# Half of each expert's second matrix product in three fp32r passes instead of native fp32

## The chip, the cores and the metric

The kernel runs on one core of a Trainium2 chip. The metric is device time in microseconds (us) of one execution. The engines named below are TensorE (PE, its weight loads PEld), VectorE (DVE), ScalarE (ACT), GpSimd (POOL) and SyncE (SP, which here only issues transfers).

## The reference

One forward pass over 512 tokens of width 1024: a first block (four token mixers, a gated merge, a mixture of experts) and then two layers of a second block. The change lies in the mixture of experts. Cut to what matters:

```python
def one_seq(xs):                                   # 512 x 1024
    lg = (xs @ wr_g) + br_g                        # 4 groups, the best is taken
    le = ((xs @ wr_e) + br_e)                      # 8 experts in the group, the best 2 are taken
    ...
    hg = jnp.einsum('sd,edh->seh', xs, w_gate)     # 32 experts, 1024 -> 256
    hu = jnp.einsum('sd,edh->seh', xs, w_up)
    h = jax.nn.silu(hg) * hu * gate[..., None]
    return jnp.einsum('seh,ehd->sd', h, w_down)    # 256 -> 1024
```

Each token has two experts with weight, so the kernel computes only those.

## The kernel before

`moe` sorts the 1024 token-expert pairs into 39 **blocks** of at most 128 rows: one per expert, and 7 overflow blocks for experts with more than 128 rows, which are empty when none has. For block b it gathers the rows (`gather`, POOL), and loads the expert's matrices from HBM: gate and up together as two chunks of 1 MB (`load_g`, chunks 2b and 2b+1), and the down matrix as one of 1 MB (`load_d`).

Products of fp32 precision are made in two ways here. Gate and up use **three fp32r passes**: each operand is split into a high part (ACT copies it with rounding to fp32r: `rounds` L1926 for weights, `round_rows` L1937 for tokens) and a low part (DVE subtracts: `split` L2103, `split_rows` L2109), and PE sums high x high, high x low, low x high (L1853 to L1855). The down product (`down`, L1867 to L1878) takes the loaded matrix as it is, in **native fp32**: two halves of 512 output columns, banks 4 and 5, each with two matmuls. A native fp32 matmul shows as two records in the trace.

Every engine runs its own list in program order; the loops over b are written out. In iteration b:

- PE: `gate_up(b)` (24 matmuls), `turn_rows(b+1)` (8 transposes, L1864), `down(b-1)`, `turn_hidden(b)` (2 transposes into bank 6, L1883). `down(b-1)` waits until ACT (`y_out_low`, L1943) and DVE (`y_out_high`, L2116) have emptied banks 4 and 5 of block b-2, since these banks are single.
- ACT: SiLU (L1961), `round_rows(b+1)`, `rounds(2b+4)`, `rounds(2b+5)`, `y_out_low(b-1)`.
- DVE: SiLU times up (`mid`, L2125), `split_rows(b+1)`, `split(2b+4)`, the copy of the turned hidden rows out of bank 6 (`hid`, L2131), `split(2b+5)`, `y_out_high(b-1)`.
- SP: `load_d(b+2)` (L1752) waits for the end of `down(b-1)`, and behind it in the queue stand the two chunks of `load_g(b+3)` (L1745). So the three 1 MB transfers of a block are issued together, just as a `down` ends; their chunks are rounded and split one iteration later.
- POOL: an indirect gather of rows three blocks ahead and a scatter of the results to HBM.

In this document a **period** runs from the end of one `down` to the end of the next; the trace marks these ends by SP's issues of L1752.

Of the kernel before, what the change touches and what calls it, by code (L numbers as in the profile page):

```python
# [38 lines left out]
OVERFLOW = 2 * SEQ // (ROWS + 1)  # L39
BLOCKS = EXPERTS + OVERFLOW  # L40
# [236 lines left out]

@contextmanager
def memory(k, **shapes):

    with ExitStack() as ctx:
        out = []
        for name, shape in shapes.items():
            dt = F32
            if shape[0] in ("r", "i"):
                dt, shape = (F32R if shape[0] == "r" else mybir.dt.int32), shape[1:]
            k.tensors += 1
            out.append(ctx.enter_context(k.nc.sbuf_tensor(f"{name}_{k.tensors}", [128, *shape], dt)))
        yield out[0] if len(out) == 1 else out
# [1382 lines left out]
def moe(k, gain1, bias1, gain2, bias2):  # L1672
# [12 lines left out]
    four = lambda name: const(k, name).rearrange("p (q e) -> p q e", q=4)  # L1685
    norm_names = norm_programs(k, k.res, gain1, bias1, k.eps[:, 0:1], True, (None,) * 5, out=k.res)[0]
    with memory(k, raw=(3, CHUNK), work=(13 * SEQ,), gh=("r", 2, KT * ROWS), gl=("r", 2, KT * ROWS), xtm=(4, D),
                router=(KT, 36), lg=(4, 36), pick=(4, 4), m=(4, 8), le=(4, 32), wide=(4, 32), hot=(2, 4, 32),
                gates=(2, 4), mask=(4, 32), rank=(4, 32), per=(4, 32), cmp=(OVERFLOW, 32), at=(6, 8),
                slot=(2, BLOCKS), stats=(4, 12), moments=(4, 4), ids=("i", 2, BLOCKS), extra=("i", 8)) as (  # L1690
            raw, work, gh, gl, xtm, router, lg, pick, m, le, wide, hot, gates, mask, rank, per, cmp, at, slot,
            stats, moments, ids, extra), \
            stage(k, "router_in", "logits_ready", "exp_ready", "best_ready", "rows_turned", "rows_out", "rows_stored",
                  "mask_ready", "ranks_ready", "places_ready", "slots_ready", "ids_ready", "vector_order",
                  "g_loaded0", "g_loaded1", "g_loaded2", "g_loaded3", "d_loaded0", "d_loaded1", "d_loaded2",
                  "g_rounded", "g_split", "g_used", "x_cleared", "gathered0", "gathered1", "gathered2",
                  "x_turned", "x_rounded", "x_split", "hidden_ready", "silu_ready", "mixed", "turned",
                  "turned_copied", "y_ready", "y_low", "y_high", "scattered0", "scattered1", "picked_in0", "picked_in1", "picked_in2", "picked_in3", "summed_y",
                  "rstd_done", "normed", "back_turned", "res_ready", "res_ready2", "tail_square_used", "tail_log_ready", "squared_rows", "params_in", *norm_names, drained=True) as (
                block, router_in, logits_ready, exp_ready, best_ready, rows_turned, rows_out, rows_stored,  # L1700
                mask_ready, ranks_ready, places_ready, slots_ready, ids_ready, order,
                g_loaded0, g_loaded1, g_loaded2, g_loaded3, d_loaded0, d_loaded1, d_loaded2,
                g_rounded, g_split, g_used, x_cleared, gathered0, gathered1, gathered2,
                x_turned, x_rounded, x_split, hidden_ready, silu_ready, mixed, turned,
                turned_copied, y_ready, y_low, y_high, scattered0, scattered1, picked_in0, picked_in1, picked_in2, picked_in3, summed_y,
                rstd_done, normed, back_turned, res_ready, res_ready2, square_used, log_ready, squared_rows, params_in, *norm_sems):
        nrm = work[:, :].rearrange("p (a n) -> p a n", n=SEQ)
        norm = norm_programs(k, k.res, gain1, bias1, k.eps[:, 0:1], True,
# [4 lines left out]
        g_hi = [ws.hi[:, 0, :], ws.hi[:, 1, :], flat(k.xh, 0), flat(k.xh, 1)]  # L1713
        g_lo = [ws.lo[:, 0, :], ws.lo[:, 1, :], flat(k.xl, 0), flat(k.xl, 1)]
        d_raw = [raw[:, 2, :], flat(k.res, 0), flat(k.res, 1)]
        g_loaded = [g_loaded0, g_loaded1, g_loaded2, g_loaded3]
        d_loaded = [d_loaded0, d_loaded1, d_loaded2]
        gathered = [gathered0, gathered1, gathered2]
        scattered = [scattered0, scattered1]
        picked_in = [picked_in0, picked_in1, picked_in2, picked_in3]  # L1720
        x_rows = [work[:, D * s:D * s + D] for s in range(3)]
        y_rows = [work[:, D * s:D * s + D] for s in (3, 4)]
# [8 lines left out]
        tile = lambda t: slice(128 * t, 128 * t + 128)  # L1731
# [82 lines left out]
        def _(pe):  # L1814
# [52 lines left out]
            def down(b):  # L1867
                pe.wait_ge(turned_copied, b + 1)
                pe.wait_ge(d_loaded[b % 3], 16 * (b // 3 + 1))
                if b:  # L1870
                    pe.wait_ge(y_low, b)
                    pe.wait_ge(y_high, b)
                for half in range(2):
                    for u in range(2):
                        last = pe.matmul(k.bank[4 + half][:, :], hid[b % 2][:, tile(u)],
                                         d_raw[b % 3][:, D * u + SEQ * half:D * u + SEQ * half + SEQ],
                                         start=u == 0, stop=u == 1)
                    last.then_inc(y_ready, 1)  # L1878
# [39 lines left out]
        def _(act):  # L1918
            def rounds(c):
                act.wait_ge(g_loaded[c % 4], 16 * (c // 4 + 1))  # L1920
                if c >= 4:
                    if c % 2:
                        act.wait_ge(hidden_ready, (c - 4) // 2 + 1)
                    else:
                        act.wait_ge(g_used, (c - 4) // 2 + 1)
                act.activation(g_hi[c % 4], g_raw[c % 4], ACT.Copy).then_inc(g_rounded, 1)  # L1926
# [5 lines left out]
            def round_rows(b):  # L1932
                for half in range(2):
# [2 lines left out]
                        act.wait_ge(hidden_ready, b - 1)  # L1936
                    act.activation(gh[:, b % 2, halves[half]], k.bank[2 + half][:, :], ACT.Copy).then_inc(x_rounded, 1)  # L1937

            def y_out_low(b):
                act.wait_ge(y_ready, 2 * b + 1)  # L1940
                if b >= 2:
                    act.wait_ge(scattered[b % 2], 16 * (b // 2))
                act.activation(y_rows[b % 2][:, 0:SEQ], k.bank[4][:, :], ACT.Copy).then_inc(y_low, 1)  # L1943
# [15 lines left out]
            for b in range(BLOCKS):  # L1959
                act.wait_ge(hidden_ready, b + 1)  # L1960
                act.activation(silu[b % 2], k.bank[b % 2][:, 0:256], ACT.Silu).then_inc(silu_ready, 1)  # L1961
                if b + 1 < BLOCKS:
                    round_rows(b + 1)
                if b + 2 < BLOCKS:
                    rounds(2 * b + 4)
                    rounds(2 * b + 5)
                if b:
                    y_out_low(b - 1)
            y_out_low(BLOCKS - 1)

            def rows_to_features(q):
# [33 lines left out]
        def _(dve):  # L2005
# [117 lines left out]
            for b in range(BLOCKS):  # L2123
                dve.wait_ge(silu_ready, b + 1)
                dve.tensor_tensor(mid[b % 2], silu[b % 2], k.bank[b % 2][:, 256:512], ALU.mult).then_inc(mixed, 1)  # L2125
                if b + 1 < BLOCKS:
                    split_rows(b + 1)
                if b + 2 < BLOCKS:
                    split(2 * b + 4)
                dve.wait_ge(turned, b + 1)  # L2130
                dve.tensor_copy(hid[b % 2], k.bank[6][:, 0:256]).then_inc(turned_copied, 1)  # L2131
                if b + 2 < BLOCKS:
                    split(2 * b + 5)
                if b:
                    y_out_high(b - 1)
            y_out_high(BLOCKS - 1)

            def rows_to_features(q):
# [519 lines left out]
def store_out(k, c0):  # L2658
    ws = k.ws
    end = c0 + LAYERS * LAYER_CHUNKS  # L2660
    with stage(k, "spare0", "spare1", "spare2", "spare3", "spare4", "spare5", "stored") as (block, _, _, _, _, _, _, stored):
        @block.sync
        def _(sp):
            sp.dma_start(k.dram["outT"], k.res[:, :, :]).then_inc(stored, 16)
            sp.wait_ge(stored, 16)
            for c in (end + 1, end + 2):
                sp.wait_ge(ws.loaded[c % SLOTS], 16 * (c // SLOTS + 1))


def build(nc, dram):  # L2670
    with ExitStack() as ctx:
        k = Kernel(nc, dram)
        k.bank = [ctx.enter_context(nc.psum_tensor(f"bank{b}", [128, 512], F32)) for b in range(8)]
        k.ws = Stream(nc, ctx, dram["weights"])
        k.xh, k.xl, k.res, k.consts, k.par1, k.par2, k.mats1, k.mats2, k.eps = ctx.enter_context(memory(
            k, xh=("r", KT, SEQ), xl=("r", KT, SEQ), res=(KT, SEQ), consts=(CONSTS,), par1=(P1_COLS,),
            par2=(P2_COLS,), mats1=(548,), mats2=(256,), eps=(5,)))
# [279 lines left out]
```

## Time and profile before

| | |
|---|---|
| median of 3 runs | 3155.22 us (3152.75 to 3158.64) |
| the profiled execution | 3157.21 us |
| its span, first to last instruction | 3155.0 us |
| granted clock of TensorE, mean | 0.942 |
| PE matmul busy, share of the span | 2813.8 us, 89% |
| DVE, ACT, POOL busy | 1752.9, 703.4, 1339.1 us |
| block loop of `moe` | about 925 to 1329 us of the span |

The profile gives for each instruction its start and length, and for the idle time ahead of it the last event that ended the wait. Busy time alone does not tell which engine sets the pace: in a loop of 39 like blocks the question is which chain of instructions and waits closes on itself once per block, and how long it is. That is read from the order in time of PE, ACT, DVE and SP.

### The profile page before, as it was taken

Reading aid. Unit: us, or ns where it says so; the run is one execution under the profiler, and the core shown is the slowest. Engines: PE = TensorE matmul, PEld = TensorE weight load, DVE = VectorE, ACT = ScalarE, POOL = GpSimd, SP = SyncE. Lnnn points to the kernel's source line nnn. Section 1 sums busy time; section 2 is a strip of 40 time slices with the busy share of each in tenths; the row PEclk is TensorE's granted clock in tenths of the full one; section 3 lists DMA queues with packets and bytes.
Section 4 is the critical chain, followed back from the end, with each engine's and each line's share of the span. In section 5 each row is a group of like instructions: output and inputs, shape, how many; then the busy total and the mean of one; then the engine's idle time right before and its main releaser. Section 6 shows DMA issues by size and latency. Waiting matters only on the chain. (4 is left out here: it accounts for less than half of the span.)

```text
span 3155.0 us, 32794 instructions
## 1 busy us (share of the span) xinstructions
PE 2813.8 (89%) x12686; PEld 2128.1 (67%) x12686; DVE 1752.9 (56%) x2031; ACT 703.4 (22%) x1082; POOL 1339.1 (42%) x382
## 2 busy tenths in 40 slices
PE   7988777879779999879889989999898899989998
PEld 6843436757556666557468867888665688768886
DVE  1176455449366666566644456882356645568841
ACT  1023220021135555452430010000233500110000
POOL 5600000036311111213147757777432277667776
PEclk9989888879979999989999999999999999999999
DMA  4322010033248888622212222222233022222223
GB/s 158 121 103 98 24 58 20 1 113 128 82 156 311 334 309 330 247 97 102 66 54 94 93 80 91 97 94 93 99 109 91 28 94 95 93 80 94 94 98 116
DMA packets 84168, 366.35 MB, mean 116 GB/s; under 512 B 32062, under 2 KB 32446, under 8 KB 45608
## 3 DMA queue, kind: packets, MB, share of 16 engines
q1 hardware_dynamic: 66088, 338.55, 29.6%
q10 hardware_dynamic: 6688, 17.21, 1.7%
q0 software_dynamic: 11232, 8.43, 0.9%
q8 instruction: 104, 1.70, 0.2%
q14 instruction: 56, 0.46, 0.0%
HBM read 364.75 MB, written 36.08 MB: 127 GB/s over the span
## 5 line engine op out<-in xcount | busy, mean ns | idle before, releaser
L177 PE MATMUL bank<-xh,w_hi 128*128 128x512 f32 x1704 | 678.1, 398 | 78.2 <-DVE xl L548 31.7
L133 POOL TENSOR_TENSOR w_hi<-w_raw,w_zero 128x2048 fp32r<-128x2048 f32 x138 | 497.5, 3605 | 588.6 <-PE bank L177 360.8
L179 PE MATMUL bank<-xh,w_lo 128*128 128x512 f32 x1704 | 670.5, 393 | 0.0
L178 PE MATMUL bank<-xl,w_hi 128*128 128x512 f32 x1704 | 670.4, 393 | 0.0
L136 POOL TENSOR_TENSOR w_lo<-w_raw,w_hi 128x2048 fp32r<-128x2048 f32 x138 | 649.5, 4706 | 10.8
L177 PEld LDWEIGHTS bank<-xh,w_hi 128*128 128x128 f32 x1704 | 324.1, 190 | 173.0 <-issue 51.7
L153 POOL TENSOR_TENSOR w_lo<-w_raw,w_hi 128x2048 fp32r<-128x2048 f32 x24 | 111.0, 4625 | 775.2 <-DVE yl L653 519.1
L179 PEld LDWEIGHTS bank<-xh,w_lo 128*128 128x128 f32 x1704 | 324.0, 190 | 68.8
L178 PEld LDWEIGHTS bank<-xl,w_hi 128*128 128x128 f32 x1704 | 324.9, 191 | 65.7 <-issue 0.5
L2649 DVE TENSOR_TENSOR fl<-work,fh 128x512 fp32r<-128x512 f32 x44 | 210.8, 4791 | 1.5
L661 DVE TENSOR_TENSOR part<-sig,bank 128x512 f32<-128x512 f32 x76 | 52.3, 688 | 251.5 <-PE bank L179 250.8
L1801 POOL DMA_INDIRECT picked_rows<-work,ids x39 | 39.2, 1005 | 327.8 <-DVE work L2116 261.4
L231 PE MATMUL bank<-whole_x,w_raw 128*128 128x512 f32 x320 | 150.7, 629 | 2.0 <-PEq L275 2.0
L723 DVE SCALAR_TENSOR_TENSOR res<-res,bank 128x512 f32<-128x512 f32 x32 | 22.0, 688 | 232.0 <-PE bank L179 232.0
L667 DVE TENSOR_TENSOR part<-part 128x512 f32<-128x512 f32 x72 | 148.1, 2057 | 2.5
L2648 DVE CAST fh<-work 128x512 fp32r<-128x512 f32 x44 | 145.7, 3312 | 1.5
L643 ACT ACTIVATE sig<-bank 128x512 f32<-128x512 f32 x76 | 45.6, 600 | 436.3 <-DVE part L661 420.4
L178 PE MATMUL bank<-fl,w_hi 128*128 128x512 f32 x352 | 137.0, 389 | 0.0
L179 PE MATMUL bank<-fh,w_lo 128*128 128x512 f32 x352 | 137.0, 389 | 0.0
L177 PE MATMUL bank<-fh,w_hi 128*128 128x512 f32 x352 | 137.0, 389 | 0.0
L2635 ACT ACTIVATE work<-bank 128x512 f32<-128x512 f32 x44 | 26.4, 599 | 437.7 <-PE bank L179 437.7
L231 PEld LDWEIGHTS bank<-whole_x,w_raw 128*128 128x128 f32 x320 | 63.5, 202 | 84.8 <-issue 84.7
(543 smaller groups left out, 4865.8 us busy)
## 6 DMA issues: line engine op xcount, KB each, us to landing
w_raw<-weights SPq DMA_DIRECT2D x216, 1024.0 KB, 4.8
raw<-weights SPq DMA_DIRECT2D x51, 1024.0 KB, 8.5
res<-weights SPq DMA_DIRECT2D x26, 1024.0 KB, 6.3
early_gates<-gate_rows SPq DMA_DIRECT2D x20, 256.0 KB, 2.1
ahead<-early_gates ACTq DMA_DIRECT2D x20, 256.0 KB, 3.5
distance_bias<-distance_bias_once ACTq DMA_DIRECT2D x8, 512.0 KB
na_bias<-grid_bias SPq DMA_DIRECT2D x16, 240.0 KB, 4.8
strips<-distance_bias SPq DMA_DIRECT2D x8, 448.0 KB, 3.9
```

The lines of the kernel that those rows point to most:

```text
L133: pool.tensor_tensor(self.hi[:, s, :], self.raw[:, s, :], self.zero[:, 0:1].to_broadcast([128, CHUNK]), ALU.add).then_inc(self.rounded, 1)
L136: pool.tensor_tensor(self.lo[:, s, :], self.raw[:, s, :], self.hi[:, s, :].bitcast(F32), ALU.subtract).then_inc(self.split, 1)
L153: engine.tensor_tensor(self.lo[:, s, :], self.raw[:, s, :], self.hi[:, s, :].bitcast(F32), ALU.subtract).then_inc(self.split, 1)
L177: self.released(pe.matmul(out, hi, moving[0], start=start, stop=False))
L178: pe.matmul(out, hi, moving[1], start=False, stop=False)
L179: return pe.matmul(out, lo, moving[0], start=False, stop=stop)
L231: mm = pe.matmul(self.k.bank[self.banks[j]][:, :], self.k.ws.raw[:, c % 2, 128 * (b % 16):128 * (b % 16) + 128], self.x[:, t, :], start=t ...
L643: act.activation(sig[:, l % 2, :], k.bank[l % 4][:, :], ACT.Sigmoid).then_inc(sigmoid_ready, 1)
L661: dve.tensor_tensor(part[:, 0 if n == 0 else 1, :], gate, k.bank[4 + u % 4][:, :], ALU.mult).then_inc(banks_free, 1)
L667: step(dve.tensor_tensor(part[:, 0, :], part[:, 0, :], part[:, 1, :], ALU.add))
L2648: step(dve.tensor_copy(fh[:, j, :], mid[:, 0, :]))
L2649: dve.tensor_tensor(fl[:, j, :], mid[:, 0, :], fh[:, j, :].bitcast(F32), ALU.subtract).then_inc(halved, 1)
```

## The change

In `down(b)` the first half (columns 0 to 511, bank 4) is computed in three fp32r passes, and the second half stays native fp32. Its operands are split per block. ACT rounds half of the down matrix, 128x1024 elements (`round_down`, into `d_hi`), and the turned hidden rows, 128x256 (`round_hidden`, into `hid_hi`). DVE subtracts both (`d_lo`, `hid_lo`). All four buffers are single, so each is written only when the first half of the `down` before has ended. `down(b)` waits for both new splits before either of its halves. The native copy `hid` stays, for the second half.

To make room, the small routing tables (`le`, `wide`, `mask`, `rank`, `per`, `hot`) become views of `work`, which is free at that time. Five semaphores move from the stage to the whole kernel, and six unused ones of `store_out` go.

```diff
+        first_half = lambda b: d_raw[b % 3].rearrange("p (u n) -> p u n", u=2)[:, :, 0:SEQ]
+        table = lambda n, w=128: work[:, 5 * D + n:5 * D + n + w].rearrange("p (q e) -> p q e", e=32)
+        le, wide, mask, rank, per = (table(128 * n) for n in range(5))
+        hot = table(640, 256).rearrange("p (a q) e -> p a q e", a=2)
...
@@ tensor: down(b)
+                pe.wait_ge(hidden_split, b + 1)
+                pe.wait_ge(d_split, b + 1)
                 for half in range(2):
                     for u in range(2):
+                        if half == 0:
+                            hh, hl = hid_hi[:, tile(u)], hid_lo[:, tile(u)]
+                            pe.matmul(k.bank[4][:, :], hh, d_hi[:, u, :], start=u == 0, stop=False)
+                            pe.matmul(k.bank[4][:, :], hh, d_lo[:, u, :], start=False, stop=False)
+                            last = pe.matmul(k.bank[4][:, :], hl, d_hi[:, u, :], start=False, stop=u == 1)
+                            continue
                         last = pe.matmul(k.bank[4 + half][:, :], hid[b % 2][:, tile(u)],
...
@@ scalar
+            def round_down(b):
+                act.wait_ge(d_loaded[b % 3], 16 * (b // 3 + 1))
+                if b:
+                    act.wait_ge(y_ready, 2 * b - 1)
+                act.activation(d_hi[:, :, :], first_half(b), ACT.Copy).then_inc(d_rounded, 1)
+
+            def round_hidden(b):
+                act.wait_ge(turned, b + 1)
+                if b:
+                    act.wait_ge(y_ready, 2 * b - 1)
+                act.activation(hid_hi[:, :], k.bank[6][:, 0:256], ACT.Copy).then_inc(hidden_rounded, 1)
...
                 if b + 2 < BLOCKS:
                     rounds(2 * b + 4)
+                round_hidden(b)
+                if b + 2 < BLOCKS:
                     rounds(2 * b + 5)
                 if b:
                     y_out_low(b - 1)
+                round_down(b)
...
@@ vector
                 dve.wait_ge(turned, b + 1)
+                dve.wait_ge(hidden_rounded, b + 1)
+                if b:
+                    dve.wait_ge(y_ready, 2 * b - 1)
+                dve.tensor_tensor(hid_lo[:, :], k.bank[6][:, 0:256], hid_hi[:, :].bitcast(F32),
+                                  ALU.subtract).then_inc(hidden_split, 1)
                 dve.tensor_copy(hid[b % 2], k.bank[6][:, 0:256]).then_inc(turned_copied, 1)
                 if b + 2 < BLOCKS:
                     split(2 * b + 5)
                 if b:
                     y_out_high(b - 1)
+                dve.wait_ge(d_rounded, b + 1)
+                dve.tensor_tensor(d_lo[:, :, :], first_half(b), d_hi[:, :, :].bitcast(F32),
+                                  ALU.subtract).then_inc(d_split, 1)
```

PE in one iteration of the block loop, before (`down` is L1875, its four native matmuls):

```order
L1864 MATMUL bank<-consts,work 128x128 x8
L1875 MATMUL bank<-res,work 128x512 x4
L1883 MATMUL bank<-consts,work 128x128 x2
L1853 MATMUL bank<-xh,gh 128x512
```

and with the change:

```order
L1868 MATMUL bank<-consts,work 128x128 x8
L1883 MATMUL bank<-d_hi,hid_hi 128x512
L1884 MATMUL bank<-d_lo,hid_hi 128x512
L1885 MATMUL bank<-d_hi,hid_lo 128x512
L1883 MATMUL bank<-d_hi,hid_hi 128x512
L1884 MATMUL bank<-d_lo,hid_hi 128x512
L1885 MATMUL bank<-d_hi,hid_lo 128x512
L1887 MATMUL bank<-raw,work 128x512 x2
L1895 MATMUL bank<-consts,work 128x128 x2
```

Two of the four native matmuls have become six fp32r ones, between the transposes of the next rows and those of the hidden rows.

ACT in one iteration, before:

```order
L1961 ACTIVATE work<-bank 128x256
L1937 ACTIVATE gh<-bank 128x512 x2
L1926 ACTIVATE xh<-raw 128x2048 x2
L1943 ACTIVATE work<-bank 128x512
```

and with the change:

```order
L1985 ACTIVATE work<-bank 128x256
L1949 ACTIVATE gh<-bank 128x512 x2
L1938 ACTIVATE xh<-raw 128x2048
L1961 ACTIVATE hid_hi<-bank 128x256
L1938 ACTIVATE xh<-raw 128x2048
L1967 ACTIVATE work<-bank 128x512
L1955 ACTIVATE d_hi<-res 128x1024
```

The rounding of the hidden rows now stands between the two weight roundings, and that of the down matrix at the end.

DVE in one iteration, before:

```order
L2109 TENSOR_TENSOR gl<-bank,gh 128x512 x2
L2103 TENSOR_TENSOR xl<-raw,xh 128x2048
L2131 COPY work<-bank 128x256
L2103 TENSOR_TENSOR xl<-raw,xh 128x2048
L2116 COPY work<-bank 128x512
L2125 TENSOR_TENSOR work<-work,bank 128x256
```

and with the change:

```order
L2136 TENSOR_TENSOR gl<-bank,gh 128x512 x2
L2130 TENSOR_TENSOR xl<-raw,xh 128x2048
L2161 TENSOR_TENSOR hid_lo<-bank,hid_hi 128x256
L2163 COPY work<-bank 128x256
L2130 TENSOR_TENSOR xl<-raw,xh 128x2048
L2143 COPY work<-bank 128x512
L2169 TENSOR_TENSOR d_lo<-raw,d_hi 128x1024
L2152 TENSOR_TENSOR work<-work,bank 128x256
```

`hid_lo` stands ahead of the copy of the hidden rows, and `d_lo`, for which PE's `down` waits, is the last of the iteration, behind both weight splits and the emptying of bank 5.

## Rows read from the trace of the kernel before

**Rows 1.** Windows: two stretches; busy us of each engine (instructions), clock, DMA share, GB/s.

```profile
980.31:1244.52 264.21, 253.66 (x1053) 176.20 (x1052) 177.14 (x175) 144.27 (x150) 50.64 (x50) 1.00 0.85 323
1244.52:1304.56 60.04, 60.04 (x254) 42.19 (x253) 43.13 (x43) 34.97 (x37) 12.16 (x12) 1.00 0.84 325
```

**Rows 2.** Timeline of PE, one `down`: start us, length us, instruction, idle before.

```profile
1110.99 0.40 PE L1855 MATMUL bank<-w_hi,gl 128*128 128x512 f32 x1
1111.22 1.04 PE L1864 MATMUL bank<-consts,work 128*128 128x128 f32 x8
1112.10 3.60 PE L1875 MATMUL bank<-res,work 128*128 128x512 f32 x8
1115.54 0.38 PE L1883 MATMUL bank<-consts,work 128*128 128x128 f32 x2
1115.67 0.47 PE L1853 MATMUL bank<-xh,gh 128*128 128x512 f32 x1
```

**Rows 3.** Timeline of SP: issues of the down matrix, the ends of `down`.

```profile
980.31 0.33 SPq L1752 DMA_DIRECT2D res<-weights  x1
...
1105.72 0.33 SPq L1752 DMA_DIRECT2D res<-weights  x1
...
1115.73 0.33 SPq L1752 DMA_DIRECT2D res<-weights  x1
...
1127.64 0.33 SPq L1752 DMA_DIRECT2D raw<-weights  x1
...
1244.52 0.33 SPq L1752 DMA_DIRECT2D res<-weights  x1
...
1304.56 0.33 SPq L1752 DMA_DIRECT2D res<-weights  x1
```

**Rows 4.** Timelines of ACT, DVE and PE around a `down` that waited.

```profile
1115.53 1.92 ACT L1926 ACTIVATE w_hi<-w_raw 128x2048 fp32r<-128x2048 f32 x1 [2.57 <-DMA w_raw<-weights]
1118.94 1.92 ACT L1926 ACTIVATE w_hi<-w_raw 128x2048 fp32r<-128x2048 f32 x1 [1.50 <-DMA w_raw<-weights]
...
1119.69 0.42 DVE L2131 COPY work<-bank 128x256 f32<-128x256 f32 x1
1120.90 2.29 DVE L2103 TENSOR_TENSOR w_lo<-w_raw,w_hi 128x2048 fp32r<-128x2048 f32 x1 [0.80 <-ACT w_hi L1926]
1123.11 0.68 DVE L2116 COPY work<-bank 128x512 f32<-128x512 f32 x1
...
1123.94 3.67 PE L1875 MATMUL bank<-raw,work 128*128 128x512 f32 x8 [1.66 <-DVE work L2116]
```

**Rows 5.** Timeline of ACT, the second weight rounding in a period without a wait.

```profile
1274.53 1.92 ACT L1926 ACTIVATE xh<-raw 128x2048 fp32r<-128x2048 f32 x1 [0.76 <-DMA raw<-weights]
```

**Rows 6.** Timelines of ACT and DVE: instructions of 256 and 1024 columns.

```profile
1121.45 0.39 ACT L1961 ACTIVATE work<-bank 128x256 f32<-128x256 f32 x1
1351.45 1.06 ACT L1981 ACTIVATE work<-res 128x1024 f32<-128x1024 f32 x1
899.59 1.22 DVE L2089 TENSOR_TENSOR work<-consts,at 128x1024 f32<-128x1024 f32 x1
```

**Rows 7.** Timelines of DVE and PE: the first `down` and the last.

```profile
932.60 0.41 DVE L2125 TENSOR_TENSOR work<-work,bank 128x256 f32<-128x256 f32 x1
932.80 3.60 PE L1875 MATMUL bank<-raw,work 128*128 128x512 f32 x8
...
1323.77 0.42 DVE L2131 COPY work<-bank 128x256 f32<-128x256 f32 x1 [2.81 <-PE bank L1883]
1324.93 3.67 PE L1875 MATMUL bank<-res,work 128*128 128x512 f32 x8 [1.21 <-DVE work L2116]
```

**Rows 8.** Timeline of PE, then windows, where the granted clock fell.

```profile
964.05 1.09 PE L1864 MATMUL bank<-consts,work 128*128 128x128 f32 x8 [1.97 <-DMA work<-token_rows,ids]
964.98 5.30 PE L1875 MATMUL bank<-raw,work 128*128 128x512 f32 x8
...
966.00:967.00 1.00, 1.00 (x2) 0.34 (x1) 0.67 (x2) 1.00 (x1) 0.69 (x2) 0.50 0.06 25
```

More of the change, by code:

```diff
@@ L1687, in moe @@
     with memory(k, raw=(3, CHUNK), work=(13 * SEQ,), gh=("r", 2, KT * ROWS), gl=("r", 2, KT * ROWS), xtm=(4, D),
[L1688 to L1692, printed above, removed]
+                router=(KT, 36), lg=(4, 36), pick=(4, 4), m=(4, 8),
+                gates=(2, 4), cmp=(OVERFLOW, 32), at=(6, 8), slot=(2, BLOCKS), stats=(4, 12), moments=(4, 4),
+                ids=("i", 2, BLOCKS), extra=("i", 8), d_hi=("r", 2, SEQ), d_lo=("r", 2, SEQ), hid_hi=("r", 256),
+                hid_lo=("r", 256)) as (
+            raw, work, gh, gl, xtm, router, lg, pick, m, gates, cmp, at, slot, stats, moments, ids, extra, d_hi, d_lo,
+            hid_hi, hid_lo), \
             stage(k, "router_in", "logits_ready", "exp_ready", "best_ready", "rows_turned", "rows_out", "rows_stored",
@@ L1695, in moe @@
                   "g_loaded0", "g_loaded1", "g_loaded2", "g_loaded3", "d_loaded0", "d_loaded1", "d_loaded2",
-                  "g_rounded", "g_split", "g_used", "x_cleared", "gathered0", "gathered1", "gathered2",
+                  "g_rounded", "g_split", "g_used", "x_cleared",
                   "x_turned", "x_rounded", "x_split", "hidden_ready", "silu_ready", "mixed", "turned",
-                  "turned_copied", "y_ready", "y_low", "y_high", "scattered0", "scattered1", "picked_in0", "picked_in1", "picked_in2", "picked_in3", "summed_y",
+                  "turned_copied", "hidden_rounded", "hidden_split", "d_rounded", "d_split", "y_ready", "y_low", "y_high", "picked_in0", "picked_in1", "picked_in2", "picked_in3", "summed_y",
                   "rstd_done", "normed", "back_turned", "res_ready", "res_ready2", "tail_square_used", "tail_log_ready", "squared_rows", "params_in", *norm_names, drained=True) as (
@@ L1702, in moe @@
                 g_loaded0, g_loaded1, g_loaded2, g_loaded3, d_loaded0, d_loaded1, d_loaded2,
-                g_rounded, g_split, g_used, x_cleared, gathered0, gathered1, gathered2,
+                g_rounded, g_split, g_used, x_cleared,
                 x_turned, x_rounded, x_split, hidden_ready, silu_ready, mixed, turned,
-                turned_copied, y_ready, y_low, y_high, scattered0, scattered1, picked_in0, picked_in1, picked_in2, picked_in3, summed_y,
+                turned_copied, hidden_rounded, hidden_split, d_rounded, d_split, y_ready, y_low, y_high, picked_in0, picked_in1, picked_in2, picked_in3, summed_y,
                 rstd_done, normed, back_turned, res_ready, res_ready2, square_used, log_ready, squared_rows, params_in, *norm_sems):
@@ L1715, in moe @@
         d_raw = [raw[:, 2, :], flat(k.res, 0), flat(k.res, 1)]
+        first_half = lambda b: d_raw[b % 3].rearrange("p (u n) -> p u n", u=2)[:, :, 0:SEQ]
+        table = lambda n, w=128: work[:, 5 * D + n:5 * D + n + w].rearrange("p (q e) -> p q e", e=32)
+        le, wide, mask, rank, per = (table(128 * n) for n in range(5))
+        hot = table(640, 256).rearrange("p (a q) e -> p a q e", a=2)
         g_loaded = [g_loaded0, g_loaded1, g_loaded2, g_loaded3]
         d_loaded = [d_loaded0, d_loaded1, d_loaded2]
-        gathered = [gathered0, gathered1, gathered2]
-        scattered = [scattered0, scattered1]
+        gathered, scattered = k.gathered, k.scattered
         picked_in = [picked_in0, picked_in1, picked_in2, picked_in3]
@@ L2660, in store_out @@
     end = c0 + LAYERS * LAYER_CHUNKS
-    with stage(k, "spare0", "spare1", "spare2", "spare3", "spare4", "spare5", "stored") as (block, _, _, _, _, _, _, stored):
+    with stage(k, "stored") as (block, stored):
         @block.sync
@@ L2674, in build @@
         k.ws = Stream(nc, ctx, dram["weights"])
+        k.gathered = [ctx.enter_context(nc.semaphore(f"gathered{n}")) for n in range(3)]
+        k.scattered = [ctx.enter_context(nc.semaphore(f"scattered{n}")) for n in range(2)]
         k.xh, k.xl, k.res, k.consts, k.par1, k.par2, k.mats1, k.mats2, k.eps = ctx.enter_context(memory(
```

## The prediction

> **What bounds the kernel now.** Only the block loop of `moe` changes, so I read that: first the windows [rows 1], then PE's timeline through one `down` [rows 2], then SP's issues, which mark the ends of the `down`s [rows 3], then ACT, DVE and PE side by side where PE waited [rows 4].
>
> In a period without a wait PE is the bound: gate and up, eight transposes, four native matmuls and two transposes follow each other without a gap, and from 1105.72 to 1115.73 that is 10.01 us [rows 2, 3]. From 1244.52 to 1304.56 six periods average 10.01 [rows 1, 3]. But the 25 periods from 980.31 to 1244.52 average 264.21 / 25 = 10.57. The next one in rows 3 shows why: 11.91 us. There the second weight chunk arrived late and ACT rounded it at 1118.94. DVE split it, then emptied bank 5 at 1123.11, and only then could `down` start, at 1123.94, after PE had waited 1.66 us [rows 4]. This `down` ended at 1127.64 [rows 3].
>
> So there is a second chain beside PE's. I write Y for the end of a `down` and r for the start of the second weight rounding counted from the Y at which that chunk was issued. In rows 4 and 3, r = 1118.94 - 1105.72 = 13.22. From there to the end of the waiting `down` are 1127.64 - 1118.94 = 8.70. It spans two periods: two periods together last at least r + 8.70. Two average ones last 2 x 10.57 = 21.14, which the chain gives at r = 12.44. The periods alternate: a short one of 10.0, where PE is the bound, and a long one of some 11.1, where the late chunk is. In the stretch without waits r is 1274.53 - 1264.53 = 10.0 (the issue lies four even periods before 1304.56 [rows 3, 5]) and the chain has 1.3 us to spare.
>
> **The change part by part.** PE: eight native records take 1115.54 - 1112.10 = 3.44, so the four of the first half take 1.72 [rows 2]. Six fp32r matmuls at 0.23 (1110.99 to 1111.22 [rows 2]) take 1.38. `down` shortens by 0.34, to 3.10, and PE's own period to 9.67. Over 39 blocks that is 13.3 us, if PE alone set the pace.
>
> The Trainium skill (page "FP8 and Floating Point Precision", section "TensorE Precision Notes") says that true fp32 goes through the array in four passes. By that rule three passes save a quarter of the half, 0.43 us, where the rows say 0.34. The sum below would be 0.1 us per block lower. The rows decide.
>
> DVE: `d_lo` is 128x1024. The nearest row of that size takes 1.22 [rows 6]; behind another instruction it adds about 1.14, as the split of 2.29 is followed 2.21 later [rows 4]. It has to stand between the emptying of bank 5 and the start of `down`, since DVE runs in order and `down` now waits for it. This is on the chain: 8.70 + 1.14 - 0.34 = **9.50**. The bounds are 0.60 (a row of half the size, 0.68, overlapped) and 1.22. I take 1.14, as the size is the same. `hid_lo`, 0.42 like the copy of its size [rows 4], adds some 0.34 ahead of the second split. In late periods DVE has 0.80 idle there [rows 4], which covers it; without that cover it would add 0.34 to a period's chain.
>
> ACT: `round_down` takes 1.06 by the row of its size [rows 6]. It follows `y_out_low` and ends, counted from the second rounding, at 1.92 + 0.5 + 1.0 = 3.4; DVE reaches `d_lo` at 4.17 + 0.60 = 4.8 [rows 4]. So it costs nothing, with 1.4 to spare. Behind it in ACT's queue is the next SiLU, which is ready at about Y + 5.7 of the next period; in late periods ACT is free just then. `round_hidden`, 0.39 [rows 6], stands ahead of the second weight rounding and waits for the turned hidden rows, which PE makes after `down`. These are there at about Y + 0.24 of the new period (transposes at 1115.54, 0.38 long, Y at 1115.73 [rows 2, 3]). That is a new tie: the second rounding can't start before Y + 0.24 + 0.29 = **Y + 0.53** (0.39, less 0.1 overlap). With the chain of 9.50 behind it, no period is shorter than 0.53 + 9.50 = **10.03**. So PE's 9.67 is never seen: a loop through ACT, DVE and PE takes its place, as long as PE's period was before.
>
> Now the late periods. A short one is 10.03 instead of 10.01. What r does there I take from before: 12.44, less 0.2, since the transfer before it now ends earlier against Y (bounds: 11.3, as in long periods, and 12.44). Two periods last 12.24 + 9.50 = 21.74, so 10.87 each instead of 10.57: **+0.30 x 25 = +7.5**. The long one is then 11.71, and its own chunk is ready before the tie lets ACT take it, so the alternation stays. The four periods ahead of 980.31: +0.8, by one such pair. The six quiet ones: 6 x 0.02 = +0.1.
>
> Start: the first `down` began at 932.80 and waited for no emptied bank; DVE ended its second split at 932.60 [rows 7]. Now `hid_lo` and `d_lo` come first: 932.60 + 0.34 + 1.14 + 0.1 = 934.2, **+1.4**, less 0.34. Take +1.1. End: after the last hidden transposes DVE copied at 1323.77 and `down` began at 1324.93 [rows 7]. Now ACT rounds (0.4), empties bank 4 (0.55) and rounds the down half (1.06), and DVE subtracts (1.22): about 1323.77 + 3.3 = 1327.1, +2.2, less 0.34: **+1.9**.
>
> The clock: once, PE waited 1.97 us and then made its transposes; in the `down` behind that the granted clock was 0.50, the 1.2 GHz level, and `down` took 5.30 instead of 3.60 [rows 8], 1.70 lost. PE's wait in a long period is now 21.74 - 10.03 - 9.67 = 2.0 each time, where it was about 1.1 before. Between none and all 13 long periods lose 1.70. The wait of 1.66 in rows 4 lost nothing (that `down` took 3.67), so I take one more loss than before: **+1.7**, bounds 0 and 22.
>
> Tables in `work`: the same DVE instructions on the same sizes, 0. Fewer semaphores to clear: some tenths at most, 0.
>
> The sum: 7.5 + 0.8 + 0.1 + 1.1 + 1.9 + 1.7 = +13.1. On the profiled execution (3157.2, 2.0 above the median) that gives 3170.3; on the median of 3155.2, **3168**.
>
> **The rivals.**
> *The saving shows.* If DVE's subtraction or ACT's tie were not on the path, each period would be 0.34 shorter: 39 x 0.34 = -13.3, 3142. DVE's busy share speaks for it (177.14 of 264.21 [rows 1]): 2 us of new work per block would fit by sum. The order in which it stands speaks against.
> *The transfers make room.* The longer chain gives the DMA more rest, and r falls. At r = 11.3 a pair needs 20.8, so 10.40 a block: -0.17 x 25 = -4.3, and with the 0.8, 0.1, 1.1 and 1.9 the total is -0.4: 3155. For it: r of long periods is lower. Against: the short period, in which the next three transfers are issued over the tail of the last, stays at 10.03. It decides at r = 11.6, where the stretch is as before.
> *The clock falls nearly every time* (slower than forecast). 13 x 1.7 = 22, with the 11.4 of the rest +33: 3189. For it: the waits of 2.0 reach the length that lost the clock once. The Trainium skill ("TensorE: Matmul & The Clock Gate", section "HAM oscillation — how this bites in real kernels") describes a loop that waited for DMA in each tile and lost the clock in each; by that rule this is the case to fear. No row here shows it twice.
>
> The side on which the forecast turns is one mechanism: whether `d_lo` is between the emptied bank and `down`. It costs 1.14 and is paid back by 0.34 in PE; from a chain slack over 0.8 on it costs nothing, and only the quiet periods have that.
>
> **How the numbers follow.** The forecast 0.58; the clock in most long periods 0.15; room in the transfers 0.17; the saving shows 0.10. About 0.2% (6.3 us) is what a measurement of this kernel can tell from no change. Of the forecast a tenth lies within that. Faster 0.12 (the saving, and a little of the room), same 0.19, slower 0.69. The range goes from 3150, below the case of room, to 3186, which takes in most of the clock's case; the saving at 3142 is left out.
>
> **What would show it.** PE's `down` about 3.1 us long: right. SP's issues no closer than 10.0 us in quiet periods, not 9.67: the loop through ACT and DVE. PE idle before `down` released by DVE's `d_lo` in most blocks, 2 us in long ones. ACT's second weight rounding never earlier than 0.5 after Y. The last `down` some 2 us later after its hidden transposes. Granted clock of 0.5 in one or two windows more. Wrong: quiet periods near 9.7, or a mean under 10.5 in the disturbed stretch.

## The result

The changed kernel is slower: 3170.81 us (median of 20 runs) against 3155.39 us (20 runs), a ratio of 1.0047 with a 95% interval of 1.0037 to 1.0056, or +11.7 to +17.7 us. The profiled execution has a span of 3166.2 us against 3155.0. The forecast was 3168.

The windows of the changed kernel, over the same 25 and 6 periods as in [rows 1] (start and end of the stretch, its length, busy us of PE, PEld, DVE, ACT, POOL, granted clock, DMA share, GB/s):

```profile
982.65:1252.58 269.93, 252.75 (x1103) 187.72 (x1102) 215.12 (x226) 176.37 (x201) 54.30 (x50) 0.98 0.83 316
1252.58:1313.98 61.40, 59.56 (x266) 44.48 (x265) 49.36 (x54) 42.08 (x48) 13.03 (x12) 1.00 0.81 315
```

The disturbed periods average 10.80 us instead of 10.57, and of the quiet ones none is below 9.97, though PE's own work had become shorter. One quiet period, by timelines of PE, ACT and DVE (start us, length us, instruction, idle before it):

```profile
1283.63 0.38 PE L1895 MATMUL bank<-consts,work 128*128 128x128 f32 x2
1289.34 1.03 PE L1868 MATMUL bank<-consts,work 128*128 128x128 f32 x8
1290.44 0.47 PE L1883 MATMUL bank<-d_hi,hid_hi 128*128 128x512 f32 x1
1293.63 0.38 PE L1895 MATMUL bank<-consts,work 128*128 128x128 f32 x2
...
1284.05 0.39 ACT L1961 ACTIVATE hid_hi<-bank 128x256 fp32r<-128x256 f32 x1 [0.86 <-PE bank L1895]
1284.33 1.91 ACT L1938 ACTIVATE xh<-raw 128x2048 fp32r<-128x2048 f32 x1
...
1286.27 2.29 DVE L2130 TENSOR_TENSOR xl<-raw,xh 128x2048 fp32r<-128x2048 f32 x1
1288.48 0.68 DVE L2143 COPY work<-bank 128x512 f32<-128x512 f32 x1
1289.08 1.22 DVE L2169 TENSOR_TENSOR d_lo<-raw,d_hi 128x1024 fp32r<-128x1024 f32 x1
```

This is the loop that the prediction names, turned once. PE's transposes of the hidden rows (1283.63) let ACT round them (1284.05); only then ACT rounds the second weight chunk (1284.33); DVE splits it, empties bank 5, makes `d_lo` to 1290.30; and `down` starts at 1290.44. The next transposes start 10.00 us after the last. `down` takes 3.19 here, from its start to that of the next transposes, against 3.44 in [rows 2] and 3.51 for the one that waited in [rows 4] (its own next transposes were at 1127.45). So a `down` after a pause takes 0.07 to 0.1 more, of either kind. Both behind a pause, the saving is 0.32; where the pause is new, 0.25 is left of it. The one `down` of the changed kernel without a pause, at 1329.69, takes 3.09 (next transposes at 1332.78), which is the 0.34 that was forecast.

What PE waited for from 930 to 1345 us, in the loop, first the kernel before, then the changed one (us in total, times, longest):

```profile
PE bank L1875 <- DVE work L2116: 11.4, 13, 1.7
PE bank L1864 <- DMA work<-token_rows,ids: 2.3, 2, 2.0
```

```profile
PE bank L1883 <- DVE d_lo L2169: 24.3, 22, 3.3
PE bank L1857 <- DVE gl L2136: 0.6, 1, 0.6
```

The wait for the emptied bank has become one for `d_lo`, more than twice as long. The longest two in mid-loop also cost clock:

```profile
1097.66 0.47 PE L1883 MATMUL bank<-d_hi,hid_hi 128*128 128x512 f32 x1 [2.23 <-DVE d_lo L2169]
...
1246.15 0.77 PE L1883 MATMUL bank<-d_hi,hid_hi 128*128 128x512 f32 x1 [2.88 <-DVE d_lo L2169]
1246.71 0.63 PE L1884 MATMUL bank<-d_lo,hid_hi 128*128 128x512 f32 x1
...
1099.00:1100.00 1.00, 1.00 (x3) 0.69 (x3) 0.76 (x2) 0.26 (x1) 0.73 (x1) 0.50 0.26 86
1247.00:1248.00 1.00, 1.00 (x4) 0.71 (x4) 0.53 (x1) 0.95 (x1) 0.81 (x1) 0.50 1.06 451
```

In both windows the clock is 0.50, the 1.2 GHz level, after waits of 2.23 and 2.88 us. The two `down`s ended 1.7 and 3.1 us later than r + 9.50 gives. A third loss, of some 1.6, is in the last `down`, after a wait of 3.3: it took 5.00 by PE's timeline, where that of the kernel before took 3.67 [rows 7].

Where the +11.2 us between the two profiled executions lie:

| part | before | changed | difference |
|---|---|---|---|
| up to the first instruction of the routing on DVE (no change there) | 879.1 | 882.7 | +3.6 |
| from there to the first SP issue that marks the end of a `down` | 57.3 | 58.6 | +1.3 |
| the 4 periods after it | 43.9 | 41.3 | -2.6 |
| 25 disturbed periods | 264.2 | 269.9 | +5.7 |
| 6 quiet periods | 60.0 | 61.4 | +1.4 |
| from there to the last emptying of bank 5 | 24.1 | 27.5 | +3.4 |
| the rest of the program (no change there) | 1826.4 | 1824.7 | -1.6 |

The first row and the last are not the change's: among the profiled executions of this study the routing starts between 878.5 and 888.1 us, and native kernels lie at both ends of that (878.7 and 887.0). The loop itself accounts for +9.2 in this pair, and that is all that this pair of traces shows of the change. The medians lie 15.4 us apart; where the rest of that lies is not shown.

### The profile page after: what moved, and what is told of

Same layout as the page of the kernel before. It is cut to its first block and busy times, and to the rows that moved or that the text cites. A ratio compares the mean times of both kernels' runs of the same rounds, so it can differ in the third digit from the quotient of the medians.

```text
span 3166.2 us, 33253 instructions
## 1 busy us (share of the span) xinstructions
PE 2811.2 (89%) x12764; PEld 2142.4 (68%) x12764; DVE 1808.3 (57%) x2109; ACT 751.6 (24%) x1160; POOL 1344.7 (42%) x382
```

## Experiments

All times are medians; the ratios are to the kernel before, timed beside. It took 3155.4 us beside the first kernels of the table, 3157.1 beside those from *tables only* to *swapped, two banks, gather ahead*, and 3155.0 beside the last four; kernels of different groups are compared by their ratios. "Disturbed" is the mean of the same 25 periods by SP's issues, "shortest" the level at which the shortest periods of the profiled execution gather.

| kernel | us | ratio, 95% interval | disturbed | shortest |
|---|---|---|---|---|
| before | 3155.4 | 1 | 10.57 | 10.00 |
| changed | 3170.8 | 1.0047 (1.0037 to 1.0056) | 10.80 | 9.98 |
| d_lo twice | 3206.9 | 1.0160 (1.0139 to 1.0182) | 11.74 | 11.24 |
| halves swapped | 3152.6 | 0.9986 (0.9972 to 0.9999) | 10.35 | 9.65 |
| native, two banks | 3159.6 | 1.0020 (1.0005 to 1.0035) | 10.65 | 10.00 |
| swapped, two banks | 3156.3 | 1.0002 (0.9991 to 1.0014) | 10.97 | 9.65 |
| tables only | 3155.2 | 0.9997 (0.9982 to 1.0012) | 10.39 | 10.00 |
| native, gather ahead | 3159.0 | 1.0011 (0.9998 to 1.0024) | 10.31 | 10.00 |
| changed, gather ahead | 3171.0 | 1.0052 (1.0032 to 1.0071) | 10.68 | 9.98 |
| swapped, two banks, gather ahead | 3146.1 | 0.9965 (0.9953 to 0.9978) | 10.14 | 9.66 |
| untied | 3178.3 | 1.0063 (1.0042 to 1.0084) | 11.05 | 9.68 |
| two passes | 3144.8 | 0.9969 (0.9956 to 0.9982) | 10.29 | 9.21 |
| native, two banks, gather ahead | 3141.6 | 0.9963 (0.9948 to 0.9978) | 10.04 | 10.00 |
| swapped, gather ahead | 3148.1 | 0.9976 (0.9962 to 0.9990) | 10.32 | 9.66 |

The mean of 25 periods comes from one execution each and differs from run to run: tables only has 10.39 where the kernel before has 10.57 at the same median. It is read for its large steps only.

**The suspected instruction twice.** The theory puts `d_lo` on the chain in every period.

```diff
                 dve.wait_ge(d_rounded, b + 1)
-                dve.tensor_tensor(d_lo[:, :, :], first_half(b), d_hi[:, :, :].bitcast(F32),
-                                  ALU.subtract).then_inc(d_split, 1)
+                for n in range(2):
+                    dve.tensor_tensor(d_lo[:, :, :], first_half(b), d_hi[:, :, :].bitcast(F32),
+                                      ALU.subtract).then_inc(d_split, 1)
+                    if n == 0:
+                        dve.wait_ge(d_split, 2 * b + 1)
...
-                pe.wait_ge(d_split, b + 1)
+                pe.wait_ge(d_split, 2 * b + 2)
```

> The changed kernel, with d_lo subtracted twice per block (the same values written again, and `down` waits for the second). Theory (the chain through DVE ends at `down`, and is always the bound): each period gets one more subtraction of 1.14 us and a semaphore round of about 0.06, so quiet periods go from 10.0 to about 11.2, and the whole to about +1.2 x 38 = +45 us over the changed kernel, some 3215. Rival (DVE's new work is mostly beside PE's, the extra time comes from elsewhere): quiet periods stay near 10.0 to 10.3 and the time within 10 us of 3171.

Measured 3206.9, +36 over the changed kernel, where +45 was expected. SP's issues in the quiet stretch:

```profile
1305.14 0.33 SPq L1756 DMA_DIRECT2D res<-weights  x1
...
1316.38 0.33 SPq L1756 DMA_DIRECT2D res<-weights  x1
...
1327.64 0.33 SPq L1756 DMA_DIRECT2D raw<-weights  x1
```

The quiet periods are now 11.25, that is 10.0 + 1.25: the full length of the subtraction. From 930 to 1345 us PE waited 35 times for `d_lo`, 53.7 us in all. The disturbed mean rose by 0.95 only, less than the sum expected: 21 of these 25 periods too are 11.2 to 11.3, so the late chunks no longer set the pace in most. In the four longer ones the clock fell, after waits of 2.5 to 3.5 us for `d_lo`. The chain is shown.

**Halves swapped.** `d_lo` beside the native half.

```diff
-                pe.wait_ge(hidden_split, b + 1)
-                pe.wait_ge(d_split, b + 1)
-                for half in range(2):
+                for half in (1, 0):
+                    if half == 0:
+                        pe.wait_ge(hidden_split, b + 1)
+                        pe.wait_ge(d_split, b + 1)
```

The waits for y_ready on ACT and DVE follow the new order.

> The changed kernel with the halves of `down` in the other order: the native half (bank 5) first, and the waits for hidden_split and d_split only ahead of the fp32r half. d_lo (1.14) then runs beside the native half (1.72). Theory: the chain falls from 9.50 to 8.36 behind the second weight rounding, the tie through ACT allows 8.9, so PE is the bound in quiet periods at 9.67, and disturbed ones average about 10.1 to 10.2 (two last r + 8.36, r about 11.9). Whole: about -10 us against the kernel before, 3145. Rival (the transfers set the pace, whatever stands behind them): disturbed periods stay at 10.5 or more and the time within 5 us of the kernel before.

Measured 3152.6, 18 us below the changed kernel, and just below the kernel before. PE's 9.67 shows for the first time: the shortest periods are 9.65. So the change's place for its wait is what made it lose. But the disturbed mean is 10.35 and not 10.1 to 10.2, and the gain is 3 and not 10 us. Up to 1310 us PE waits for three things. Against the changed kernel the gathered rows are new, and the emptied bank 5 (L2144) is back; the kernel before had both:

```profile
PE bank L1868 <- DMA work<-token_rows,ids: 6.8, 6, 3.7
PE bank L1888 <- DVE work L2144: 6.4, 9, 1.2
PE bank L1857 <- DVE gl L2137: 0.6, 1, 0.6
```

L1868 turns the gathered rows: they come late.

The chain can be read off each kernel, as the shortest time from the second weight rounding (ACT's timeline) to the end of the `down` behind it (SP's). In the 25 disturbed periods it is 8.69 before, 9.49 with the change, 10.74 with `d_lo` twice and 8.37 with the halves swapped, where 8.70, 9.50, about 10.7 and 8.36 were forecast.

**Two banks, native and swapped.** The emptying of bank 5 out of the chain.

```diff
                 if b:
                     pe.wait_ge(y_low, b)
-                    pe.wait_ge(y_high, b)
+                if b > 1:
+                    pe.wait_ge(y_high, b - 1)
...
-                        last = pe.matmul(k.bank[4 + half][:, :], hid[b % 2][:, tile(u)],
+                        last = pe.matmul(k.bank[4 + half * (1 + 2 * (b % 2))][:, :], hid[b % 2][:, tile(u)],
...
-                dve.tensor_copy(y_rows[b % 2][:, SEQ:D], k.bank[5][:, :]).then_inc(y_high, 1)
+                dve.tensor_copy(y_rows[b % 2][:, SEQ:D], k.bank[5 + 2 * (b % 2)][:, :]).then_inc(y_high, 1)
```

> The kernel before, all native, with one edit: the second half of `down` goes to bank 5 and bank 7 in turn, so that `down` waits for the emptying of two blocks ago. Theory (the late periods of the kernel before are the chain weight chunk, rounding, split, emptied bank 5, `down`): the chain is cut, every period is PE's 10.01, PE has no wait ahead of `down`, and the time falls by 0.56 x 25 = 14 us plus the lost clock, to about 3140. Rival (the transfers can't deliver three chunks each 10.0 us): PE waits elsewhere, for g_split or gathered rows, and the mean period stays near 10.5.

> Both edits on the changed kernel: halves swapped and the native half in bank 5 and 7 in turn. Theory: nothing of the chain is left ahead of PE, periods are 9.67, whole 39 x 0.34 = 13 us below the two-bank kernel of native products: about 3127. Rival (the transfers are the floor then): the mean period in the disturbed stretch stays at or over 10.0 and the time is near that of the two-bank native kernel, about 3140.

Both missed. The native one took 3159.6, no gain at all, the swapped one 3156.3. PE's waits, native and then swapped:

```profile
PE bank L1864 <- DMA work<-token_rows,ids: 11.2, 7, 3.6
```

```profile
PE bank L1868 <- DMA work<-token_rows,ids: 18.2, 10, 3.2
PE bank L1885 <- DVE d_lo L2171: 3.0, 5, 1.0
```

The wait for the bank is gone up to 1310 us, as meant, and the time went into another: the gathered rows. With them went clock: behind such waits it fell to 0.50 in two places of the native kernel and in five of the swapped one. On POOL the gather of block b+4 stands behind the scatter of block b, and that waits until both banks of block b are emptied, at the end of DVE's iteration. With `down` no longer held back, the gather is what comes last. So the rival was right that something of the transfers sets the pace. That it is not their throughput at 10.0 us a period is shown by the all-native kernel with two banks and the gather ahead, below.

**Tables only.** The other half of the change by itself.

> The changed kernel without the three-pass product: only the routing tables inside `work`, the buffers for the splits reserved but unused, and the semaphores moved. Theory: this part costs nothing, 3155 within 3 us; the 15 us are all the product's. Rival (the layout or the cleared semaphores cost something): a part of the +15 shows here, 3 us or more.

3155.2: the tables, buffers and semaphores cost nothing, within 0.2%.

**The gather ahead.** One edit on POOL, on three kernels.

```diff
-            for b in range(3):
+            for b in range(4):
                 gather(b)
             for b in range(BLOCKS):
-                if b + 3 < BLOCKS:
-                    gather(b + 3)
+                if b + 4 < BLOCKS:
+                    gather(b + 4)
                 scatter(b)
```

> The kernel before with one edit on POOL: the gather of block b+4 is issued ahead of the scatter of block b, so that it no longer waits behind that block's emptied banks. Theory (in the kernel before, late weight chunks and the emptied bank 5 are the bound, gathers only once): the time falls by at most the one lost clock and that wait, 0 to -5 us. Rival (gather and scatter sent as a pair delay the weight chunks): r falls clearly in the disturbed stretch and the time by 8 us or more.

> The same edit on the changed kernel. Theory (its bound is the chain through d_lo): within 4 us of 3171. Rival (late gathered rows take part in its loss): 3163 or less.

> Halves swapped, two banks, and the gather ahead. In the profile of the swapped two-bank kernel PE waits 17.6 us ahead of the turning of rows for gathered rows. Theory: with the rows fetched a block earlier this wait goes and PE's 9.67 shows in nearly every period: about 3125 to 3132. Rival (the transfers as a whole are the floor): the wait moves to the weight chunks, the mean disturbed period stays at 10.3 or more and the time at 3145 or more.

On the kernel before the edit alone gives nothing (3159.0, ratio 1.0011, where 0 to -5 us was expected), on the changed kernel nothing (3171.0, as expected). On the swapped kernel with two banks it gives 10 us, to 3146.1, without reaching the expected 3125 to 3132. The waits for gathered rows are gone there, and in the profile `down` waits for `d_lo` again:

```profile
PE bank L1885 <- DVE d_lo L2171: 9.2, 13, 1.5
```

One such case. ACT waited for the chunks, and DVE behind it:

```profile
1022.66 1.92 ACT L1940 ACTIVATE xh<-raw 128x2048 fp32r<-128x2048 f32 x1 [3.48 <-DMA raw<-weights]
1025.73 1.92 ACT L1940 ACTIVATE xh<-raw 128x2048 fp32r<-128x2048 f32 x1 [0.89 <-DMA raw<-weights]
...
1027.68 2.29 DVE L2132 TENSOR_TENSOR xl<-raw,xh 128x2048 fp32r<-128x2048 f32 x1
1030.50 1.21 DVE L2171 TENSOR_TENSOR d_lo<-raw,d_hi 128x1024 fp32r<-128x1024 f32 x1
...
1031.85 0.47 PE L1885 MATMUL bank<-d_hi,hid_hi 128*128 128x512 f32 x1 [1.51 <-DVE d_lo L2171]
```

The chunk rounded at 1025.73 is needed by PE only two blocks later. It delays this block because `d_lo`, which this block needs, stands behind its split in DVE's list.

**Untied, and two passes.** The two parts of the new loop apart.

```diff
@@ untied: scalar
                 if b + 2 < BLOCKS:
                     rounds(2 * b + 4)
-                round_hidden(b)
-                if b + 2 < BLOCKS:
                     rounds(2 * b + 5)
+                round_hidden(b)
...
@@ untied: round_hidden
-                act.activation(hid_hi[:, :], k.bank[6][:, 0:256], ACT.Copy).then_inc(hidden_rounded, 1)
+                act.activation(hid_hi[:, :], hid[b % 2], ACT.Copy).then_inc(hidden_rounded, 1)
...
@@ untied: vector
+                dve.wait_ge(hidden_rounded, b + 1)
+                dve.tensor_tensor(hid_lo[:, :], hid[b % 2], hid_hi[:, :].bitcast(F32),
+                                  ALU.subtract).then_inc(hidden_split, 1)
                 dve.wait_ge(d_rounded, b + 1)
                 dve.tensor_tensor(d_lo[:, :, :], first_half(b), d_hi[:, :, :].bitcast(F32),
...
@@ two passes: tensor
-                            pe.matmul(k.bank[4][:, :], hh, d_lo[:, u, :], start=False, stop=False)
-                pe.wait_ge(d_split, b + 1)
+                pe.wait_ge(d_rounded, b + 1)
```

> The changed kernel, but the hidden rows are rounded from their copy in `work` behind the second weight rounding, and hid_lo is made just ahead of d_lo. Theory (two bounds in the changed kernel: the tie of the second rounding to the end of `down`, and the chain behind it): without the tie quiet periods fall from 10.0 to (10.0 + 9.50 + 0.34) / 2 = 9.92, since the chain is now 9.84 behind r; disturbed ones stay near 10.7; whole within 5 us of 3171. Rival (the tie is the main cost): quiet periods reach 9.67 and the time falls under 3162.

> The changed kernel without d_lo and its pass: the product of the high hidden rows with the low part of the matrix is left out, ACT still rounds both, DVE makes hid_lo alone, and `down` waits for ACT's d_rounded. Theory: the chain falls by 1.14 and another 0.46 of PE, to 7.9, quiet periods are PE's 9.67 - 0.46 = 9.21, the disturbed mean about 10.1, the whole 3132 to 3142. Rival (ACT's new roundings cost by themselves, or the transfers do not allow it): 3155 or more.

Untied took 3178.3, more than the 5 us around 3171 that were expected. Its interval (1.0042 to 1.0084) overlaps that of the changed kernel, so that it is slower is not shown; that the tie is not the main cost is. Without it `hid_lo` too stands ahead of `down`: single periods of 9.67 do occur, but pairs last at least r + 9.82, as expected (r + 9.84). In its profile the clock fell in four places, in that of the changed kernel in three.

Two passes leave out the product with `d_lo` and its subtraction, and keep ACT's roundings. The kernel took 3144.8, above the expected 3132 to 3142, and its disturbed mean is 10.29 and not 10.1, with 12.6 us of waits for gathered rows. Quiet periods go down to PE's 9.21, as expected, so in those ACT's new work costs nothing. How much of the 26 us is DVE's subtraction and how much PE's missing pass (0.46 a block) this kernel can't tell; what a subtraction costs is shown by *d_lo twice*.

**The counterparts of the fastest.**

> The kernel before with the second half of `down` in bank 5 and 7 in turn and the gather ahead, all native. It is the counterpart of the fastest so far, which has the three-pass half. Theory (PE's saving of 0.34 a block counts once nothing else waits): quiet periods 10.01, disturbed about 10.3, 3150 to 3156, 4 to 10 us above the three-pass one's 3146. Rival (the three passes give nothing even then, all of its gain is from banks and gathers): within 2 us of 3146.

> The changed kernel with the halves swapped and the gather ahead, bank 5 single. Theory: the emptied bank 5 is back in the chain (8.36 behind r), so disturbed periods average 10.3 where two banks have 10.1: 3148 to 3152. Rival (the second bank gives nothing): within 2 us of 3146.

The all-native kernel with two banks and the gather ahead has the lowest median of all: 3141.6, 0.9963 (0.9948 to 0.9978). Here the expectation of 3150 to 3156 missed and the rival held. The three-pass kernel with the same two edits has 0.9965 (0.9953 to 0.9978), timed in another group: the two can't be told apart, and the three passes give nothing once the other waits are gone. The native kernel's windows row, and PE's only wait from 938 to 1300 us:

```profile
980.00:1240.00 260.00, 259.83 (x1090) 182.12 (x1089) 183.06 (x183) 149.42 (x157) 52.67 (x52) 1.00 0.88 340
...
PE bank L1876 <- issue: 0.2, 1, 0.2
```

PE is busy 259.83 of 260 us, and 21 of the 25 periods are 10.0, the longest 10.41. Weight chunks were later than ever: r averages 12.62 over the 25 periods, against 11.83 before, and one chunk was rounded 14.07 after its Y, against 13.22 in [rows 4]. It cost nothing, since nothing that the next `down` needs stands behind its split any more. The last kernel, swapped with bank 5 single, took 3148.1, in the expected range; the second bank is worth the difference to 3146.1, which the intervals don't separate.

The all-native counterpart of this last kernel is the one with the gather ahead alone, at 1.0011 (0.9998 to 1.0024). Against it 0.9976 (0.9962 to 0.9990) is a gain of 0.35%, and the intervals don't overlap. So with bank 5 single the three passes do pay, if `d_lo` is out of the chain: the chain with the emptied bank is then 8.37 and not 8.69, the 0.34 that PE saves. Part of that gain could be the order of the halves itself; a native kernel with its halves swapped was not run.

## Why the prediction was right

**The bound before** (PE in quiet periods, late chunk and single bank 5 in the others): right. The native kernel with two banks and the gather ahead has PE alone as its bound, and its 25 periods average 10.04 where they averaged 10.57. What the prediction missed is that a third wait, the gathered rows, lay just below. It did not matter for the change, which left them alone.

**PE's saving**, 0.34 a block, never seen: right in both. In size it is 0.35 without a pause (3.44 to 3.09), and 0.25 to 0.32 where `down` waited (3.19). The estimate from the four passes that the Trainium skill states (page "FP8 and Floating Point Precision", section "TensorE Precision Notes") was 0.43, further off.

**The chain**, 8.70 + 1.14 - 0.34 = 9.50: one case, from the second rounding at 995.66 to the end of `down` at 1005.23, is 9.57, and 19 of the 25 are 9.49 to 9.54.

```profile
995.66 1.92 ACT L1938 ACTIVATE w_hi<-w_raw 128x2048 fp32r<-128x2048 f32 x1 [0.61 <-DMA w_raw<-weights]
...
1005.23 0.33 SPq L1756 DMA_DIRECT2D raw<-weights  x1
```

The doubled subtraction shows that its term counts in full.

**The tie and the shortest period**, 0.53 + 9.50 = 10.03: measured 10.0, from 0.36 (1284.33 after the Y of 1283.97) and 9.64. The two errors cancel.

**The disturbed periods**, +0.30 each, +7.5: measured +0.23, +5.7, of which 4.7 are lost clock (the 1.7 and 3.1 above, less rounding). So by this estimate only some +1 is the chain itself. The term that was mis-sized is r. The forecast took 12.24 for the short periods, with long ones of 11.71 in turn with them. But the chain ended 19 of the 25 pairs, at a mean r of 11.46, and only the periods that lost clock were longer than 11.71. Before, it had ended 12, at a mean r of 12.46. The second chunks landed earlier: 11.33 us after their Y in the mean of the 25, where it had been 11.81. The medians from issue to landing, before and then with the change:

```profile
raw<-weights SPq DMA_DIRECT2D x32, 1024.0 KB, 8.5
w_raw<-weights SPq DMA_DIRECT2D x26, 1024.0 KB, 9.2
```

```profile
raw<-weights SPq DMA_DIRECT2D x32, 1024.0 KB, 8.3
w_raw<-weights SPq DMA_DIRECT2D x26, 1024.0 KB, 8.7
```

This is the rival "the transfers make room". It was half right, and the clock took its gain back.

**The other periods**, +0.8 and +0.1: measured -2.6 and +1.4. In the four, the kernel before had its one lost clock, behind the wait of 1.97 for gathered rows [rows 8], in a period of 13.88, and the changed kernel had neither. Also, one pair at +0.30 each is 0.6, not 0.8. The six quiet ones of the changed kernel hold one of 11.39, behind the longest of the disturbed.

**The clock**, +1.7 with bounds 0 and 22: in the profiled pair three losses, some 6.4 us in all, against one of 1.7, so +4.7. It is spread over the parts above and below. The rival that put a loss in nearly each long period did not come. Only two waits ahead of the last `down` were over 2 us.

**Start and end**, +1.1 and +1.9: +1.3, and +3.4. Of the 3.4, 2.05 are the later start of the last `down` behind its hidden transposes (3.64 us, where it was 1.59; forecast +2.2), and 1.3 its greater length, in which the clock took some 1.6 and the three passes gave back 0.3:

```profile
1332.78 0.38 PE L1895 MATMUL bank<-consts,work 128*128 128x128 f32 x2
...
1336.42 0.47 PE L1883 MATMUL bank<-d_hi,hid_hi 128*128 128x512 f32 x1 [3.26 <-DVE d_lo L2169]
```

**Tables**, 0: right, by the kernel with them alone.

The sum was +13.1; the medians say +15.4, with +11.7 to +17.7 as interval, and the loop of the profiled pair +9.2. The mechanism held. That the size came out near is in part luck: a term too large (r) stood beside one too small (the clock).

**The rivals.** *The saving shows*: refuted by the shortest periods. The saving is real, though: with the wait behind the native half 9.65 appears.

## What to carry to other kernels

An engine that works its list in order turns a late input into a delay of everything behind it: here a weight chunk needed two blocks later held back the emptying of a bank, and with the change the operand that the next product waits for. Before moving work to an engine with free time, look at where in its list the work must stand and who waits behind it, and put the consumer's wait as late as its own independent work allows.

And cure waits together: a second bank alone gave nothing (3159.6), an earlier gather alone nothing (3159.0), both 13 us (3141.6). A wait that vanishes only uncovers the next one. The three passes, shorter than native ones, paid where they shortened a chain that set the pace (0.9976 against 1.0011), and not where PE alone set the pace of the native kernel (0.9965 against 0.9963): there `down` still waited 9.2 us for `d_lo`, and some chunks were late enough for that.

## What the runs showed of the hardware

A 128x512 native fp32 product takes 0.86 us and three fp32r passes 0.69 in a stream of matmuls, so three passes save a fifth. After a pause a `down` of either kind takes 0.07 to 0.1 more (3.51 for 3.44, 3.19 for 3.09).

TensorE's granted clock fell to 0.50 after waits of 2.23 and 2.88 us behind eight transposes, after one of 3.26 behind two, and after one of 1.97 ahead of eight [rows 8]. The wait of 1.66 us in [rows 4] lost nothing. Each loss cost 1.6 to 3.1 us. The length of the wait alone doesn't decide. One of 1.88 us lost the clock in the swapped kernel with two banks, and one of 2.70 did not in the swapped kernel with the gather ahead:

```profile
1188.94 1.09 PE L1868 MATMUL bank<-consts,work 128*128 128x128 f32 x8 [1.88 <-DMA work<-token_rows,ids]
...
1190.00:1191.00 1.00, 1.00 (x3) 0.42 (x2) 0.74 (x2) 1.00 (x3) 0.70 (x1) 0.50 0.81 312
```

```profile
1197.45 1.96 PE L1888 MATMUL bank<-res,work 128*128 128x512 f32 x4 [2.70 <-DVE work L2144]
...
1198.00:1199.00 1.00, 1.00 (x5) 0.52 (x3) 1.00 (x3) 0.18 (x1) 0.84 (x1) 1.00 0.34 139
```

What does decide between 1.9 and 2.7 us, these runs leave open.

Three 1 MB loads each 10.0 us, with gathers and scatters beside them, are sustained at 340 GB/s and a DMA share of 0.88 in the all-native kernel with two banks and the gather ahead. So the throughput of the transfers was not the bound of the kernel before, at 323 GB/s [rows 1]. Whether they could keep up at 9.67 us a period for long is not shown.
